# Sampled attention scores from two products a head, with high and low query parts in one stationary tile, and GpSimd taking part in the splits

## What is computed

```python
def diff_logits(q, q_pos, k, k_pos, rel_bias):
    s = jnp.einsum('bqhmd,bkhmd->bhmqk', q, k).astype(jnp.float32) * (HEAD_DIM ** -0.5)
    ...
    s = s + bias[None, :, None]
    return jnp.where((dist >= 0)[None, None, None], s, -1e30)

def diff_weights(logits, lam):
    p = jax.nn.softmax(logits, axis=-1)
    return p[:, :, 0] - lam * p[:, :, 1]

def sample_attn(q, k, v, lam, k_past, v_past, rel_bias):
    ...
    w = diff_weights(jnp.concatenate([s_past, s_new], axis=-1), lam).astype(v.dtype)
    return (jnp.einsum('bhqk,bkhe->bqhe', w[..., :past], v_past)
            + jnp.einsum('bhqk,bkhe->bqhe', w[..., past:], v))
```

## Time and profile before

| what | value |
| --- | --- |
| median of 3 runs | 2070.19 us (2068.45 to 2070.83) |
| the profiled execution | 2068.8 us, of which the profile's span is 2066.9 us |
| PE busy over the span | 98% |
| DVE, ACT, POOL busy over the span | 67%, 48%, 1% |
| the rounds of the sampled stage | about 842 to 1108 us of the span |

### The profile page before, as it was taken

How to read it: one execution, slowest core, us unless ns; L and a number is a source line. 1 busy time by engine, 2 the same in 40 slices (tenths; PEclk the granted TensorE clock), 3 DMA queues, 4 the chain that set the end, 5 groups by cost and what they waited for, 6 DMA issues and landing times. The chain is left out here.

```text
span 2066.9 us, 36364 instructions
## 1 busy us (share of the span) xinstructions
PE 2020.3 (98%) x12096; PEld 1880.8 (91%) x12096; DVE 1386.9 (67%) x3022; ACT 991.8 (48%) x1824; POOL 12.4 (1%) x42
## 2 busy tenths in 40 slices
PE   7999999999999999899999999999999999999998
PEld 6999999999999999888987899999999898989896
DVE  6766676767676766688885467575757574847476
ACT  5757575757575747677774333231313131413133
POOL 0000000000000000000000000000000000000000
PEclk9999999999999999999999999999999999999999
DMA  6411111112111112787782121111202020202012
GB/s 201 138 57 53 56 52 56 58 54 58 49 58 50 58 51 86 293 287 271 284 279 89 58 81 52 36 58 32 62 22 72 22 72 22 62 22 70 12 52 98
DMA packets 167421, 183.01 MB, mean 89 GB/s; under 512 B 11077, under 2 KB 139621, under 8 KB 167317
## 3 DMA queue, kind: packets, MB, share of 16 engines
q1 hardware_dynamic: 166105, 180.98, 27.0%
q10 hardware_dynamic: 1212, 0.81, 0.1%
HBM read 162.56 MB, written 24.46 MB: 90 GB/s over the span
## 5 line engine op out<-in xcount | busy, mean ns | idle before, releaser
L1247 PE MATMUL ps<-h_hi,w_hi 128*128 128x384 f32 (+1 forms) x1152 | 386.5, 336 | 10.2 <-DVE v_lo L1170 6.8
L1247 PE MATMUL ps<-h_hi,w_lo 128*128 128x384 f32 (+1 forms) x1152 | 376.6, 327 | 0.0
L1247 PE MATMUL ps<-h_lo,w_hi 128*128 128x384 f32 (+1 forms) x1152 | 376.4, 327 | 0.0
L2333 PE MATMUL ps<-h_hi,f_w_hi 128*128 128x320 f32 (+1 forms) x1136 | 370.7, 326 | 0.8 <-PEq L1532 0.8
L2333 PE MATMUL ps<-h_hi,f_w_lo 128*128 128x320 f32 (+1 forms) x1136 | 370.4, 326 | 0.0
L2333 PE MATMUL ps<-h_lo,f_w_hi 128*128 128x320 f32 (+1 forms) x1136 | 370.2, 326 | 0.0
L2412 ACT ACTIVATE yc<-ps,f_prm 128x384 f32<-128x384 f32 x144 | 93.5, 654 | 553.8 <-PE ps L2333 391.0
L2313 PE MATMUL ps<-d_hi,act 128*128 128x512 f32 x816 | 257.1, 390 | 1.6 <-DVE d_lo L2516 1.6
L1247 PEld LDWEIGHTS ps<-h_hi,w_hi 128*128 128x128 f32 x1152 | 217.4, 189 | 13.5 <-DVE v_lo L1170 7.2
L1247 PEld LDWEIGHTS ps<-h_lo,w_hi 128*128 128x128 f32 x1152 | 217.0, 188 | 0.6
L1247 PEld LDWEIGHTS ps<-h_hi,w_lo 128*128 128x128 f32 x1152 | 216.7, 188 | 0.0
(11 more groups left out here) (308 smaller groups left out, 3585.3 us busy)
## 6 DMA issues: line engine op xcount, KB each, us to landing
k<-in_cache_k SPq DMA_DIRECT2D x64, 512.0 KB, 5.9
v_raw<-in_cache_v SPq DMA_DIRECT2D x64, 512.0 KB, 4.6
w_raw<-in_w_in SPq DMA_DIRECT2D x48, 512.0 KB, 4.0
f_raw<-in_w_up SPq DMA_DIRECT2D x48, 512.0 KB, 4.0
f_raw<-in_w_down SPq DMA_DIRECT2D x24, 512.0 KB, 3.5
bias<-bias_tiles_dram SPq DMA_DIRECT2D x8, 576.0 KB, 3.7
merged_dram<-mg SPq DMA_DIRECT2D x8, 544.0 KB, 2.7
ow_raw<-in_w_out SPq DMA_DIRECT2D x8, 512.0 KB, 6.4
```

Of the source, the lines that this page charges most:

```text
L1247: last_ = pe.matmul(bank(s)[:, 0:n], w[:, W_SLOT[g], k, :], x[:, k, off:off + n], start=(k == 0 and i == 0), stop=(k == KT - 1 and i == 2))
L2333: l_ = pe.matmul(ps[:, e % 6, 0:n], w[:, p, k, :], x[:, k, off:off + n], start=(k == 0 and i == 0), stop=(k == KT - 1 and i == 2))
```

## The change

It does six things.

1. Queries: high and low parts stand in one stationary tile `qd`. For heads 0 to 3 the high parts fill columns 0 to 63 and the low parts 64 to 127; for heads 4 to 7 it is the other way round. A chunk then takes two products, with `kt_hi` and with `kt_lo`, 6 a head and 48 a round. The low x low part comes along.
2. So `S3` holds the high rows of four heads and, apart from them, their low rows. After head 3 and after head 7, ACT copies the 64 low rows to SBUF (`low_rows`), and DVE adds them to the 64 high rows into `P` (`sum_rows`). PE may not start head 4, nor head 0 of the next round, before that. The bias and maximum instruction then reads `P` from SBUF.
3. New keys are split once for all sequences (`kn`); POOL copies 2 x 8 columns per head into `kt` (`new_key`). New values are split once (`vn`, high in partitions 0 to 63, low in 64 to 127), and their page takes 2 products over 128 partitions in place of 4 over 8; POOL copies the new weights into `p_new` at each round (`new_weights`).
4. Of the low parts of the value pages, POOL makes those of pages 2, 5 and 7.
5. The pages' splits and products are placed anew (`SPLIT_AT`, `PV_AT`, `PV_EARLY`).
6. ACT's `copy_o2` comes ahead of the exponential, the queries of the next sequence are prepared in two halves, and in round 8 `fold_rows` comes one step earlier.

```diff
-SPLIT_AT = {2: (0,), 3: (1,), 4: (2, 3), 5: (4, 5), 6: (6,), 7: (7,)}
-PV_AT = {4: (0, 1), 5: (2, 3), 6: (4, 5), 7: (6, NPAGES), 8: ()}
+HH = H // 2
+SPLIT_AT = {2: (0, 1), 3: (2, 3), 5: (4, 5), 6: (6,), 7: (7,)}
+PV_EARLY = {5: (2,)}
+PV_AT = {4: (0, 1), 5: (3,), 6: (4,), 7: (5,), 8: (6, NPAGES)}
+POOL_PAGES = (2, 5, 7)
...
+            def new_key(b, h):
+
+                if at_start(b) and h == 0:
+                    pool.wait_ge(new_lo, 1)
+                if not (at_start(b) and h < 2):
+                    pool.wait_ge(qkh_done, 8 * b + h - 1)
+                    pool.sem_inc(settled, 1)
+                pool.tensor_copy(kt[:, :, h % 2, PAST:NKEYS], kn[:, :, h, bass.ds(DEC_T * b, DEC_T)])\
+                    .then_inc(ktn_done, 1)
...
+            def body(b, u):
+                for h in range(H):
+                    if has(b, 0):
+                        new_key(b, h)
+                    if h == 2 and has(b, 1):
+                        new_weights(b)
+                    if has(b, 1):
+                        for n in splits_of(b).get(h, ()):
+                            if n in POOL_PAGES:
+                                pool.wait_ge(vhi_done, 8 * (b - 1) + n + 1)
+                                pool.tensor_tensor(v_lo[:, n, :], v_raw[:, n, :], v_hi[:, n, :].bitcast(F32),
+                                                   ALU.subtract).then_inc(vplo_done, 1)
...
+                    if has(b, 1):
+                        for n in PV_EARLY.get(h, ()):
+                            page(b, n)
                     if h >= 1 and has(b, 0):
                         g = h - 1
                         if g == 0:
                             if not at_start(b):
-                                pe.wait_ge(ttr_done, b)
+                                pe.wait_ge(sum_done, 2 * b)
                             pe.wait_ge(qdlo_done, 4 * b + 2)
-                        if g == H - 2:
+                        if g == HH:
+                            pe.wait_ge(sum_done, 2 * b + 1)
                             pe.wait_ge(qdlo_done, 4 * b + 4)
...
-                            for x, (q, k) in enumerate(((qd_hi, kt_hi), (qd_hi, kt_lo), (qd_lo, kt_hi))):
-                                last = pe.matmul(S3[:, cc, :], q[:, 128 * g:128 * (g + 1)], k[:, g % 2, keys],
-                                                 start=(g == 0 and x == 0), stop=(g == H - 1 and x == 2))
+                            for x, k in enumerate((kt_hi, kt_lo)):
+                                last = pe.matmul(S3[:, cc, :], qd[:, 128 * g:128 * (g + 1)], k[:, g % 2, keys],
+                                                 start=(g % HH == 0 and x == 0), stop=(g % HH == HH - 1 and x == 1))
...
+            def low_rows(b, s):
+
+                hi, lo = half_rows(s)
+                act.wait_ge(qkh_done, 8 * b + HH * (s + 1))
+                act.activation(slo[hi, :].rearrange("p (a n) -> p a n", a=3), S3[lo], ACT.Copy)\
+                   .then_inc(slo_done, 1)
...
+            def sum_rows(b, s):
+
+                hi, _ = half_rows(s)
+                dve.wait_ge(slo_done, 2 * b + s + 1)
+                dve.tensor_tensor(P[hi, :].rearrange("p (a n) -> p a n", a=3), S3[hi],
+                                  slo[hi, :].rearrange("p (a n) -> p a n", a=3), ALU.add).then_inc(sum_done, 1)
...
                 if has(b, 0):
-                    dve.wait_ge(qkh_done, 8 * b + 8)
...
-                    dve.tensor_tensor_reduce(out=P[:, :].rearrange("p (a n) -> p a n", a=3), in0=S3,
...
+                    sum_rows(b, 1)
+                    dve.wait_ge(sum_done, 2 * b + 2)
+                    dve.sem_inc(settled, 1)
+                    dve.tensor_tensor_reduce(out=P[:, :], in0=P[:, :], in1=sbias[:, :], scale=1.0, scalar=-3e38, op0=ALU.add, op1=ALU.max,
```

203 lines of the change are left out of this document (116 added, 87 removed).

## The result

| what | before | after |
| --- | --- | --- |
| median | 2070.51 us (2068.45 to 2071.72, 6 runs) | 2078.47 us (2077.24 to 2081.90, 6 runs) |
| ratio to before, 95% interval | | 1.0042 (1.0029 to 1.0055) |
| the profiled execution, its span | 2068.8 us, 2066.9 us | 2081.9 us, 2080.1 us |
| mean granted clock of TensorE in the profile | 0.998 | 0.991 |

The account below looks back on a forecast made before the run. PE, busy 98%, was taken as the bound. Round terms +1.3, -2.5, -15.5, -1.5 and -0.4 gave -18.6 us; +4.2 for the collision made -14.4, say 2056 us, range 2048 to 2066.

Parts of the forecast that it names:

- PE's prices: Per step on PE: 8 transposes 0.87 us, score products 0.159 us each, page products 0.233 us each.
- the walk: Full round worked out step by step across engines: 27.3 us with about 1.8 of waits, a gain of 3.1 us.
- PE's list: PE's own work in a full round, summed without waits: 25.4 us against 30.4 before.
- PE's wait in step 2: Before step 2's transposes, PE waits for DVE to end the previous keys: 0.6 us, and 0.15 for the second bank.
- POOL's page: POOL's subtraction for one value page: 2.3 us taken, covered for pages 2, 5 and 7 even at 2.8.
- the ceiling of 36 us: Whole sampled stage: the gain if no engine waited anywhere, 8 x (3.8 + 0.65) us; not the forecast.
- a partial slowing: POOL's page 2 beside DVE's page 3: 0.6 us taken between nothing and 1.4, +4.2 us over seven rounds.
- the full collision: Rival: POOL's page 2 holds DVE's page 3 until it ends, 1.4 us in seven rounds; 2061 us, chance 0.22.
- nearly none of the 3.8 us comes ... +1.3: Round 0, without pages as cover: +1.0 for copy and sum before head 4, +0.3 for splitting the new keys.
- Key loads start some 3 us later ... No cost: DMA: key loads start later because page 6 is multiplied later, with more than 15 us until needed; no cost.
- then nothing else is late: Round 8: after fold_rows moves a step earlier, 5.6 us of output products stand before PC; -0.4 us.
- POOL is too slow: Rival: POOL's pages last 3.5 us or more, so the gain is gone; 2079 us at 4 us, chance 0.13.

Follow-up runs that it names:

- e2: Changed kernel with POOL filling the low parts of value pages 2, 5 and 7 with zeros in place of subtracting; 2059.64 us, 0.9952.
- e5: Changed kernel with value page 3 split in step 4, behind the weights' low part, in place of step 3; 2061.70 us, 0.9958.
- e7: Changed kernel with page 3 and round 8's pages 2 to 5 split a step later, new value rows split in round 1, output rows loaded before output weights; 2053.38 us.
- e16: Kernel before the change without its third score product (low queries with high keys), nothing added for it; 2052.50 us, 0.9909.
- e4: Changed kernel with three filler products on PE, read by nobody, ahead of page 0 in rounds 1 to 7; 2076.51 us, 1.0033.
- e13: Changed kernel with one filler product on PE ahead of the transposes of step 2 and one ahead of those of step 3; 2075.06 us, 1.0025.
- e10: Kernel before the change with four unused sums on DVE ahead of the weights' low part in rounds 1 to 7; 2084.15 us, 1.0067.
- e1: Changed kernel with the new value rows split in round 1, step 6, in place of round 0; 2080.34 us, 1.0047.
- e15: Changed kernel with the first tile of output rows loaded ahead of the output weights in round 7; 2076.79 us, 1.0035.
- e3: Changed kernel with all low parts of the value pages made by DVE, none by POOL; 2066.65 us, 0.9983.
- e9: Changed kernel with page splits and products placed as before the change, all pages on DVE; 2065.25 us, 0.9978.

## Why the prediction was wrong

**What held.** PE's prices: a step with one page takes 2.75 us, 0.87 + 0.95 + 0.93 as forecast. A full round without a collision: 27.3 forecast, 27.56 in e2, which keeps the walk's order (e5 and e7, with page 3 later, have 27.62). That this is so near is partly luck: e2's waits are 1.25 us a round where the walk had 1.8, and the rest of the round is 0.8 longer than in the walk. The prediction's own numbers showed 0.55 of that: 30.4 less the 4.45 saved is 25.95, and PE's list has 25.4. PE's wait in step 2: 0.75 forecast, 0.75 measured. POOL's page: 2.3 taken, 2.42 measured (mean of 6), covered in steps 5 to 8 as worked out. PE waits for the sum of rows in round 0, not in full rounds. And the ceiling of 36 us stays far off: in the old order the saved products alone bring 17 of their 30.5 (e16).

**The collision, the term that I sized by choice.** The prediction took 0.6 us between nothing and 1.4, "a partial slowing". It is 1.33 to 1.39, every time, in rounds 1 to 7. There is no partial slowing: one instruction waits for nearly the whole of the other. Here the page of the Trainium skill that the prediction named (SBUF — State Buffer, Who interferes with whom) had it right (its words on the whole instruction stand beside the two-port modes; the 2.58 us show it for this subtraction too), and I gave its rival 0.22 because no row could show it. This is 0.75 us more in each of seven rounds, and it is the smaller half of what the collision did (5.2 us in all; e2, whose POOL only fills, is 18.8 us faster): by the walk alone the full collision gives 2061 us.

**The clock, which is in no step.** The walk counts a wait of PE at its own length. In the changed kernel, PE stands still for 2.4 to 2.8 us in a full round (1.75 to 1.96 of it ahead of page 0), and in three of five full rounds the clock falls to 0.50 behind it, 1.5 us each: 4.6 us of the 10.0 missed in rounds 2 to 6. Another 3.8 are the collision, and the remaining 1.6 are 0.3 a round by which the walk itself was short. e4 and e13 show that the falls need PE's standing still, by filling part of it; in e10 a lone wait of 1.6 to 1.9 us brought none in seven rounds.

**Round 0: "nearly none of the 3.8 us comes ... +1.3".** Missed by 5.2 us. The step that failed is the sum of this round: it has a term for "the split of the new keys ahead of head 0" and none, nor a reason for none, for the split of the new values in step 7. What I didn't ask is when its data arrive. They are issued behind eight key pages and land 5.15 us after ACT wants them. e1 puts it at 4.2 us; on average the maximum of round 0 starts at 871.9 us in eight profiles with this split in round 0 and at 868.3 in six without, 3.6 us. Another 0.8 us lies ahead of the stage.

**Round 7: "Key loads start some 3 us later ... No cost", -1.5 us.** Missed by 7.7 us. The sentence holds for the key loads. It passes over the rows that are loaded behind the output weights in this round, whose place in SP's queue moved back with them: 2.0 us in e15's profile, with one stretch of half clock less, and 1.2 between e5 and e7. The rest is page 3 in a round in which DVE has no slack: held by POOL's page and ahead of the weights, PE standing still for 5.1 us, the clock at 0.50 from 1065 to 1071.6 us. Page 3 a step later takes 5.7 us off (e5), the collision alone 4.1 (e2).

**Round 8: "then nothing else is late".** Missed by 3.2 us. I looked at pages 5 and 7 on POOL as covered, and they are; but POOL's subtractions hold DVE's pages in round 8 too, 7.91 us for three, and PE stands still for 2.6 us with a fall of the clock behind it. Without POOL's pages the same round takes 27.1 us (e3), against 28.1 forecast.

**POOL.** The rival "POOL is too slow" named the right engine and the right sign, but by a duration above 3.5 us. It measured 2.42. The way to the other side was not POOL's time but what it did to DVE, and what PE's waiting then did to PE. POOL's copies of the new keys had no price either; queued behind its pages they keep PE for 1.1 us in round 7, and for 0.4 a full round in e5. None of my rivals had two effects of one cause in a row, and all five pieces, missed by 1.3 to 10 us, lie on one side.

**What stays open.** Why rounds 2 and 3 of the changed kernel keep the clock with the same waits with which rounds 4 to 6 lose it, why e1, with the same waits, loses it in all of them, and why e3 keeps it with 2.1 to 2.5 us of idle time a round where e9 lost it once with 1.9. Several waits near each other against one, and the total of them, were not set apart.

## What to carry to other kernels

A subtraction with both inputs in SBUF must not stand on VectorE, on the path, beside one on GpSimd: look for the pair in the order of the instructions, and move one by a step before anything else (one number here, 17 us). When an almost full TensorE gets less work, count each new wait not only at its length, but ask whether the waits bring its clock down; a version with filler products tells this for the price of one run. And a split that is moved earlier needs a look at when its data land and at what else stands behind the moved loads.

## What the runs showed of the hardware

- TensorE, busy for 27.2 of 30 us, still lost its clock: the granted clock fell to 0.50 for some 3.5 us in rounds with waits of 2.4 to 2.8 us together, at a cost of 1.5 us each, and once with 1.9 us (e9), while a lone wait of 1.6 to 1.9 us in each of seven rounds (e10) never did this. The same program had rounds with and without a fall at equal waits.
- Products that nobody reads didn't make the kernel slower but rather faster: the medians lie 2.0 us (e4) and 3.4 us (e13) below that of the changed kernel, the full rounds 0.4 and 0.9 us shorter, with intervals of the ratios that overlap.
- VectorE's subtraction with both inputs in SBUF (1.22 us) waits for nearly the whole of GpSimd's (2.39 us): it takes 2.58 us when it starts 0.90 after it. Beside GpSimd's fill it takes no longer (3.55 us for three against 3.49), nor does a subtraction that reads PSUM, beside GpSimd's subtraction (0.69 against 0.68).
- GpSimd suffers as well: 2.39 us a page in the full rounds, 3.20 in round 8 beside VectorE's pages, and its copy of 16 elements a partition takes 0.20 us alone and up to 1.3 where it falls beside VectorE's page.
